# The scans' opening moved into attention's last units: maxima spread, four weight blocks split, head 0's value projections

## The chip, the cores and the metric

The kernel runs on one core of one Trainium2 chip. Its time is the device time of one launch in microseconds (us). Matrix products run on TensorE (PE; its weight loads are shown as PEld), elementwise work and reductions on VectorE (DVE), activations and scaled copies on ScalarE (ACT), some products and masks on GpSimd (POOL), and the transfers are issued by SyncE (SP). PSUM is the eight-bank memory that PE writes (512 fp32 columns a bank), SBUF the working memory.

## The reference

One trunk layer of a hybrid diffusion backbone on 128 context tokens and 1024 latent tokens, model width 1024: a SwiGLU half step, a token mixer, a second SwiGLU half step, each with modulation and a closing layer norm. The change lies in the mixer. It projects its input once and splits the columns into an attention part (8 query heads, 2 key/value heads of 64) and a part for four recurrent heads of 128 (HGRN2, run forward and backward):

```python
def mixer_latent(h, *, k_ctx, v_ctx, s_f0, s_b0, w_in, w_out, q_g, k_g, hg_g, lb_f, lb_b):
    hq, hi, hff, hfb, hgate, aq, ak, av = split_in(h @ w_in)
    o_hg, _, _ = hgrn2_mixer(hq, hi, hff, hfb, hgate, lb_f, lb_b, hg_g, s_f0, s_b0)
    q, k, v = attn_proj(aq, ak, av, q_g, k_g)
    ...
    o_att = block_attention(q, k_all, v_all)
    y = jnp.concatenate([o_hg, o_att.astype(o_hg.dtype)], axis=-1) @ w_out

def hgrn2_mixer(hq, hi, hf_fwd, hf_bwd, hgate, lb_fwd, lb_bwd, norm_g, s_fwd0, s_bwd0):
    q = heads(jax.nn.silu(hq.astype(f32)))
    v = heads(hi.astype(f32))
    # per direction: f = lb + (1 - lb) * sigmoid(hf); gated linear recurrence in chunks of 16 over (q, 1 - f, log f, v)
    ...
    o = rms_norm(o_f + o_b, norm_g.reshape(HG_HEADS, HG_HEAD_DIM)).reshape(b, l, HG_WIDTH)
    o = o * jax.nn.silu(hgate.astype(f32))
```

## The kernel before

The kernel keeps all 1152 tokens in SBUF as nine tiles of 128 and runs in phases, each a block of five hand-written instruction queues: the first half step with the mixer's query, key and value projection and attention, then the scans with the output projection, then the last half step. At the end of a block all engines meet; nothing of the next block runs before that. Within a block the order on each engine is that of the code, and semaphores (`wait_ge`, `then_inc`) tie the engines together.

**Attention** goes through 18 units u (nine query tiles by two key/value heads, `NU` = 18). Units 0 to 15 are latent tiles over ten key tiles; 16 and 17 belong to the context tile and have one key tile each. The queues are pipelined over units: in the iteration of unit u, PE transposes the probabilities of u (`turn`), multiplies them with the values (`values`), computes the scores of u + 1 (`main`, `tails`) and the first of u + 2, and spreads the inverse sums (`inverse_rows`). ACT exponentiates (`exponents`), copies the transposes out as high halves (`probs_hi`), and at the end the inverse rows and the low half of the output (`copy_rows`, `low_half`). DVE takes the minima of the scores (`least`), the low halves (`probs_lo`) and adds the output halves (`add_halves`, semaphore `added`), which PE's next unit and POOL's closing product (L1428) wait for. The transposes share two banks, so each waits for the low half of the one two before. The scores use the first five banks; the context units' scores touch banks 0 and 3 alone.

**The scans** need, for each head, five weight blocks of 128 columns: V (values), F0 and F1 (forget gates of the two directions), Q, and G (output gate). Products are in fp16 in three passes, so each fp32 block is split: the largest absolute value of all partitions gives a power of two, ACT writes the scaled high half (L3070, semaphore `w_hi`), DVE the low half (L3236, `w_lo`). Head 0's blocks are loaded during attention (`load_scan_weights`), and its five per-partition maxima are taken there too (`next_weight_max`, in units 12, 13, 14, 16, 17). At the opening of the scans' block PE spreads the maxima over the partitions (`spread_max`'s form, L2886), DVE reduces them and makes scale and inverse (`power`), the splits V, F0, Q, F1 follow, and PE runs `project`: V in nine units of one tile (24 products of 128 columns each, L2903), the others in three units of 384 columns (24 products each, L2906). Each unit goes to one of two banks, in the order of `ring`, and waits (`left`) until ACT has evacuated the unit two before (L3057 for V, L3061 for the others). For the next head SP loads each raw block as soon as `w_lo` shows the previous split, sends the maxima through DRAM to spread them (`spread_max` on SP: L2800 out, L2802 back), and loads G behind that; DVE's `row_max` waits for four loads at once. ACT's queue has `split(1, V_)`, which waits for head 1's scales (`w_scale`), between the gates' logarithm and Q's evacuations:

```python
            split(0, G_)
            evacuate(0, F0, 0, 1, 2)
            log_gate(0, 0)
            split(1, V_)
            evacuate(0, Q_, 0, 1, 2)
            exps(0, 0)
```

PE's queue in the scans begins with the spread and then waits for `ready`, which POOL raises when it has written zero states, the reset row and two masks (L2843 to L2856).

## Time and profile before

| | us |
|---|---|
| median of 3 runs | 2631.96 |
| lowest and highest run | 2628.84 and 2632.33 |
| the profiled execution, its own time | 2627.32 |
| span of the profiled execution (first to last instruction) | 2625.6 |
| mean granted TensorE clock, share of full speed | 0.97 |

In a row of a timeline the columns are the start, the length, the engine, the line of the kernel, the operation with output and inputs, and its count; in brackets how long the engine stood idle before it, and what ended that. Rows with a count over one merge instructions in a run. The clock column of a stretch is 1.00 at 2.4 GHz and 0.50 at 1.2 GHz.

### The profile page before, as it was taken

What the parts mean: (1) busy time and instruction counts of PE and PEld (TensorE: products, weight loads), DVE (VectorE), ACT (ScalarE), POOL (GpSimd) and SP (SyncE); (2) the same over time, 40 slices, a digit from 0 to 9 for tenths busy, and PEclk for the clock granted to TensorE, in tenths of its full rate; (3) what the DMA queues carried; (4) which work ended last, traced back from release to release, by engine and by line L of the source; (5) the groups of instructions that cost most, each with busy time, mean ns of one, the idle gap of its engine ahead of it and who ended that gap; (6) DMA issues with size and microseconds to landing.
All of it is one profiled execution on the core that took longest, in us unless ns stands there. A gap on an engine that the chain in (4) does not pass through costs nothing. (4 is left out here: it accounts for less than half of the span.)

```text
span 2625.6 us, 38449 instructions
## 1 busy us (share of the span) xinstructions
PE 2451.6 (93%) x15508; PEld 1500.0 (57%) x15508; DVE 1925.7 (73%) x2867; ACT 827.6 (32%) x1313; POOL 186.5 (7%) x220
## 2 busy tenths in 40 slices
PE   7999999999999787999799889899899999999987
PEld 2555555555555466777576666545455555555543
DVE  4687777789576766888648658798877676677687
ACT  2411111111121345777644454623222121122220
POOL 0000000000000022222200000311000000000002
PEclk9999999999999889999899999899999999999998
DMA  8133322331212111000120111231211111111001
GB/s 329 49 113 97 97 83 94 97 113 62 67 36 85 63 37 27 1 1 1 31 67 15 42 45 37 69 102 49 65 48 48 48 33 47 48 48 38 26 25 65
DMA packets 151085, 160.55 MB, mean 61 GB/s; under 512 B 11767, under 2 KB 128403, under 8 KB 149922
## 3 DMA queue, kind: packets, MB, share of 16 engines
q1 hardware_dynamic: 150946, 158.61, 19.1%
q8 instruction: 98, 1.61, 0.3%
q14 instruction: 41, 0.34, 0.0%
HBM read 148.47 MB, written 10.12 MB: 60 GB/s over the span
## 5 line engine op out<-in xcount | busy, mean ns | idle before, releaser
L2010 PE MATMUL psum<-act_hi,ffn_win_hi 128*128 128x384 f16 x2064 | 675.2, 327 | 4.8 <-DVE ffn_win_lo L2334 2.4
L2010 PE MATMUL psum<-act_lo,ffn_win_hi 128*128 128x384 f16 x2064 | 674.8, 327 | 0.0
L2010 PE MATMUL psum<-act_hi,ffn_win_lo 128*128 128x384 f16 x2064 | 674.7, 327 | 0.0
L2210 ACT ACTIVATE ffn_silu<-psum,ffn_win_inverse 128x384 f32<-128x384 f32 x132 | 76.3, 578 | 1061.5 <-PE psum L2010 1057.8
L2402 DVE SCALAR_TENSOR_TENSOR Y<-psum,ffn_h_unit,Y 128x512 f32<-128x512 f32 x324 | 239.8, 749 | 108.2 <-PE psum L2055 106.2
L2055 PE MATMUL psum<-ffn_wout_hi,ffn_h_hi 128*128 128x512 f16 x720 | 278.1, 386 | 7.5 <-issue 5.3
L2010 PEld LDWEIGHTS psum<-act_hi,ffn_win_hi 128*128 128x128 f16 x2064 | 202.5, 98 | 139.1 <-DVE ffn_win_lo L2334 2.8
L2010 PEld LDWEIGHTS psum<-act_hi,ffn_win_lo 128*128 128x128 f16 x2064 | 202.5, 98 | 134.7 <-issue 2.0
L2010 PEld LDWEIGHTS psum<-act_lo,ffn_win_hi 128*128 128x128 f16 x2064 | 202.5, 98 | 133.9 <-issue 1.5
L2055 PE MATMUL psum<-ffn_wout_lo,ffn_h_hi 128*128 128x512 f16 x720 | 277.7, 386 | 0.0
L2055 PE MATMUL psum<-ffn_wout_hi,ffn_h_lo 128*128 128x512 f16 x720 | 277.2, 385 | 0.0
L2367 DVE SCALAR_TENSOR_TENSOR ffn_h_even<-psum,ffn_win_inverse,ffn_silu 128x384 f32<-128x384 f32 x72 | 44.2, 614 | 123.5 <-ACT ffn_silu L2210 123.3
L2055 PEld LDWEIGHTS psum<-ffn_wout_hi,ffn_h_hi 128*128 128x128 f16 x720 | 71.7, 100 | 97.3 <-issue 10.9
L2906 PE MATMUL psum<-act_hi,scan_w_hi 128*128 128x384 f16 x384 | 125.4, 326 | 0.0
L2906 PE MATMUL psum<-act_lo,scan_w_hi 128*128 128x384 f16 x384 | 125.2, 326 | 0.0
L2906 PE MATMUL psum<-act_hi,scan_w_lo 128*128 128x384 f16 x384 | 125.2, 326 | 0.0
L2190 ACT ACTIVATE ffn_win_hi<-ffn_win_raw,ffn_win_scale 128x2048 f16<-128x2048 f32 x44 | 87.7, 1994 | 115.9 <-DVE ffn_win_inverse L2328 90.0
L429 DVE SCALAR_TENSOR_TENSOR mod_sums<-w_mod,silu_cond,mod_sums 128x1024 f32<-128x1024 f32 x98 | 122.8, 1277 | 0.0
L2055 PEld LDWEIGHTS psum<-ffn_wout_hi,ffn_h_lo 128*128 128x128 f16 x720 | 71.5, 99 | 88.1 <-issue 5.7
L1343 DVE TENSOR_REDUCE score_min<-psum 128x1 f32<-128x1280 f32 (+1 forms) x72 | 97.5, 1354 | 33.1 <-PE psum L1136 22.2
L1355 DVE TENSOR_TENSOR probsT_lo<-psum,probsT_hi 128x512 fp32r<-128x512 f32 x162 | 105.5, 683 | 19.7 <-ACT probsT_hi L1274 19.5
L2055 PEld LDWEIGHTS psum<-ffn_wout_lo,ffn_h_hi 128*128 128x128 f16 x720 | 71.6, 99 | 83.3 <-issue 4.6
(379 smaller groups left out, 4298.3 us busy)
## 6 DMA issues: line engine op xcount, KB each, us to landing
ffn_win_raw<-in_w_in SPq DMA_DIRECT2D x88, 512.0 KB, 5.1
w_mod<-in_w_mod SPq DMA_DIRECT2D x36, 1024.0 KB, 5.0
ffn_wout_raw<-in_w_out SPq DMA_DIRECT2D x44, 512.0 KB, 4.1
scan_w_raw<-in_w_mix SPq DMA_DIRECT2D x20, 512.0 KB, 5.3
x_after<-Y SPq DMA_DIRECT2D x9, 512.0 KB, 2.6
mixout_residual<-x_after SPq DMA_DIRECT2D x9, 512.0 KB, 3.5
Y<-in_x_sample SPq DMA_DIRECT2D x8, 512.0 KB, 11.6
ffn_residual<-in_x_sample SPq DMA_DIRECT2D x8, 512.0 KB, 3.3
```

The costliest lines, as they stand in the source:

```text
L429: ins = nc.vector.scalar_tensor_tensor(acc, w, factor, acc, ALU.mult, ALU.add)
L1343: self.nc.vector.tensor_reduce(self.low[:, u % 2, s:s + 1], self.score_view(u, s), AX_X, ALU.min).then_inc(self.s_min, 1)
L1355: nc.vector.tensor_tensor(self.pt[g % self.NPT][1][:], self.T[i % 2], self.pt[g % self.NPT][0][:].bitcast(F32), ALU.subtract).then_inc(sel ...
L2010: last = nc.tensor.matmul(bank[:, 0:CH], win[b][w][:, half, k, :], K.A[a][:, k, c * CH:(c + 1) * CH], start=(n == 0), stop=(n == 3 * KT - 1))
L2055: last = nc.tensor.matmul(py[m % 3], h[a][:, b, t * P:(t + 1) * P], wout[w][:, b, 0 if mod else int(t == CTX_T), half * 512:(half + 1) * 512],
L2190: nc.scalar.activation(win[par][0][:], wraw[par][:], ACT.Copy, scale=ws[:, par:par + 1]).then_inc(in_hi, 1)
L2210: nc.scalar.activation(sa[s][:], pa[s][:, 0:CH], ACT.Silu, scale=winv[:, b:b + 1]).then_inc(silu, 1)
L2367: nc.vector.scalar_tensor_tensor(dst, pu[s][:, 0:CH], winv[:, b:b + 1], sa[s][:], ALU.mult, ALU.mult).then_inc(hprod, 1)
L2402: ins = nc.vector.scalar_tensor_tensor(dst, py[m % 3], hq[:], dst, ALU.mult, ALU.add)
L2906: last = nc.tensor.matmul(proj[u % 2][:, 0:CH], w[x][:, k, :], K.A[y][:, k, i * CH:(i + 1) * CH], start=(m == 0), stop=(m == 3 * KT - 1))
```

## The change

Head 0's opening is taken out of the scans' block, except for block G and the evacuation of the values, and put into attention's last units.

- The maxima of blocks 3 and 4 (Q and G) are taken by DVE in unit 14, right behind that of block 2, in place of units 16 and 17.
- In unit 15 PE spreads the five maxima (`spread_weights`) into banks 1 and 2 ahead of the scores' tail; at the unit's end DVE computes the scales (`next_weights_scale`), ACT the high half of V and DVE its low half.
- In unit 16 PE projects value tiles 0 and 1, 2 and 3, 4 and 5 at three places of its order, in unit 17 tiles 6 and 7 and then 8 (`next_values`), into banks 1, 2 and 4. ACT splits Q, F1's and F0's high halves behind `low_half` of unit 16 (blocks 2, 3, 1), DVE their low halves at the end of its unit 16.
- In the scans' block PE begins with `ready` and F0. ACT evacuates the nine value tiles in three copies (`v_first`), for which F0's second unit waits. `w_lo`, `w_hi` and `w_scale` are raised at once, so SP's loads for head 1 no longer wait for head 0's splits.
- The split weights and the scales get fixed places in SBUF outside what attention uses.

```diff
@@ -1055,6 +1055,8 @@
         self.s_main, self.s_tail, self.s_min, self.ex, self.inverse = (
             sem(n) for n in ("scores", "score_tails", "score_min", "exp", "inverse"))
         self.pv, self.low_out, self.added, self.scaled = sem("pv"), sem("low_copied"), sem("o_added"), sem("o_scaled")
+        self.next_spread, self.next_scale, self.next_hi, self.next_lo, self.next_chain = (
+            sem(n) for n in ("scan_w_spread", "scan_w_scaled", "scan_w_hi", "scan_w_lo", "scan_w_chain"))
         self.next_in, self.next_late, self.next_max = sem("scan_w_loaded"), sem("scan_w_late"), sem("scan_w_max")
         self.tiles = [len(self.keys(u)) for u in range(self.NU)]
         self.first = [sum(self.tiles[:u]) for u in range(self.NU + 1)]
@@ -1164,6 +1166,50 @@
             pe.wait_ge(self.ex, h)
         self.scores(u, 2 * pair, 1024, 1024, 256)
         self.scores(u, 2 * pair + 1, 1280, 0, 256).then_inc(self.s_tail, 1)
+
+    def spread_weights(self, pe):
+
+        K = self.K
+        pe.wait_ge(self.next_max, 5)
+        pe.wait_ge(self.ex, NKV * CTX_T * self.HPK)
+        for b in range(5):
+            last = spread_max(self.nc, K, K.first_spread[:, b * P:(b + 1) * P], K.scan_rmax[:, b:b + 1])
+        last.then_inc(self.next_spread, 1)
+
+    def next_values(self, pe, *tiles):
+
+        K, (hi, lo) = self.K, self.K.scan_W[0]
+        for i in tiles:
+            if i == 0:
+                pe.wait_ge(self.next_lo, 1)
+            bank, n = K.first_v[i // 4][:, (i % 4) * P:(i % 4 + 1) * P], 0
+            for k in range(KT):
+                for x, y in PASSES:
+                    self.nc.tensor.matmul(bank, K.A[x][:, k, i * P:(i + 1) * P], (hi, lo)[y][:, k, :], start=(n == 0), stop=(n == 3 * KT - 1))
+                    n += 1
+
+    def next_weights_hi(self, act, *blocks):
+
+        K = self.K
+        for b in blocks:
+            act.wait_ge(self.qkv.q_steps, self.qkv.ROPE * NT)
+            act.wait_ge(self.next_scale, 1)
+            self.nc.scalar.activation(K.scan_W[b][0][:], K.scan_raw[:, b], ACT.Copy, scale=K.first_ws[:, b:b + 1]).then_inc(self.next_hi, 1)
+
+    def next_weights_lo(self, dve, n, b):
+
+        K = self.K
+        dve.wait_ge(self.next_hi, n + 1)
+        self.nc.vector.scalar_tensor_tensor(K.scan_W[b][1][:], K.scan_raw[:, b], K.first_ws[:, b:b + 1], K.scan_W[b][0][:],
+                                            ALU.mult, ALU.subtract).then_inc(self.next_lo, 1)
+
+    def next_weights_scale(self, dve):
+
+        K, nc, link = self.K, self.nc, Chain(dve, self.next_chain)
+        dve.wait_ge(self.next_spread, 1)
+        link(nc.vector.tensor_reduce(K.first_wmax, K.first_spread.rearrange("p (j q) -> p j q", q=P), AX_X, ALU.max))
+        power_of_two(nc, link, K.first_wmax, K.first_wq, K.first_ws)
+        nc.vector.tensor_scalar(K.first_winv, K.first_wq, K.unit_a[:, 1:2], None, ALU.mult).then_inc(self.next_scale, 1)
 
     def tensor(self, pe):
 
@@ -1216,19 +1262,31 @@
             main(pe, u + 1, 2)
             turn(u, 4)
             turn(u, 5)
+            if u == NU - 3:
+                self.spread_weights(pe)
             tails(pe, u + 1, 1)
+            if u == NU - 2:
+                self.next_values(pe, 0, 1)
+            if u == NU - 1:
+                self.next_values(pe, 6, 7)
             values(u, 0)
             values(u, 1)
             turn(u, 6)
             turn(u, 7)
             values(u, 2)
             main(pe, u + 1, 3)
+            if u == NU - 2:
+                self.next_values(pe, 2, 3)
             values(u, 3)
             values(u, 4)
             self.turn_queries(pe, u + 2)
             turn(u, 8)
             values(u, 5)
             inverse_rows(u)
+            if u == NU - 2:
+                self.next_values(pe, 4, 5)
+            if u == NU - 1:
+                self.next_values(pe, 8)
             main(pe, u + 2, 0)
             tails(pe, u + 2, 0)
             turn(u, 9)
@@ -1311,7 +1369,11 @@
             probs_hi(u + 1, 0)
             self.exponents(act, u + 2, 0)
             probs_hi(u + 1, 1)
+            if u == NU - 3:
+                self.next_weights_hi(act, 0)
             low_half(u)
+            if u == NU - 2:
+                self.next_weights_hi(act, 2, 3, 1)
 
     def keys_lo(self, dve, kv, b):
 
@@ -1401,8 +1463,15 @@
             self.least(dve, u + 2, 0)
             if u in (12, 13, 14):
                 next_weight_max(u - 12)
-            elif u in (16, 17):
-                next_weight_max(u - 13)
+                if u == 14:
+                    next_weight_max(3)
+                    next_weight_max(4)
+            if u == NU - 3:
+                self.next_weights_scale(dve)
+                self.next_weights_lo(dve, 0, 0)
+            elif u == NU - 2:
+                for n, b in ((1, 2), (2, 3), (3, 1)):
+                    self.next_weights_lo(dve, n, b)
         add_halves(NU - 1)
 
     def pool(self, gp):
@@ -2652,9 +2721,10 @@
     with ExitStack() as ctx:
         sem = lambda n: K.semaphore(f"scan_{n}")
         raw, rmax = K.scan_raw, K.scan_rmax
-        W = [[place(f"scan_w_{s}_{x}", [P, KT, P], F16) for x in ("hi", "lo")] for s in range(5)]
+        W = K.scan_W
+        place.at += 5 * 4096
         wmax, wq = place("scan_w_max", [P, 5]), place("scan_w_unit", [P, 5])
-        ws, winv = ([place(f"scan_w_{n}_{i}", [P, 5]) for i in range(2)] for n in ("scale", "inverse"))
+        ws, winv = ([first, place(f"scan_w_{n}", [P, 5])] for n, first in (("scale", K.first_ws), ("inverse", K.first_winv)))
         spread = place("scan_w_max_spread", [P, 5 * P])
         q = place("scan_q", [P, TOK])
         reset = place("scan_reset", [P, CH])
@@ -2693,7 +2763,7 @@
         stored, chain, pchain = sem("states_stored"), sem("chain"), sem("pool_chain")
         mix_in = [sem(f"mixout_w_loaded_{i}") for i in range(3)]
         mix_parts = ((0, 2, 3), (1, 4), (5, 6, 7))
-        first_max, w_turned = K.wide[3][:, 0:5 * P], sem("first_w_max_spread")
+        v_first = sem("first_v")
         w_max, w_stored, w_spread, w_scale = sem("w_max"), sem("w_max_stored"), sem("w_max_loaded"), sem("w_scaled")
         wv = K.w_mix[0].rearrange("(k p) n -> p k n", p=P)
 
@@ -2705,7 +2775,7 @@
         RPH = 6
         CPT = P // SCAN
 
-        ring = [(0, b, i) for b in (V_, F0, Q_, F1) for i in range(COUNT[b])]
+        ring = [(0, b, i) for b in (F0, Q_, F1) for i in range(COUNT[b])]
         for h in range(HGH):
             n = h + 1
             parts = [[(n, V_, i) for i in range(6)], [(h - 1, "norm", i) for i in (2, 1, 0)], [(n, V_, i) for i in range(6, NT)],
@@ -2882,10 +2952,6 @@
 
         @block.tensor
         def _(pe):
-            for b in range(NBLK):
-                last = nc.tensor.matmul(first_max[:, b * P:(b + 1) * P], rmax[:, b:b + 1].broadcast_to([P, P]), K.ident[:],
-                                        start=True, stop=True)
-            last.then_inc(w_turned, 1)
             pe.wait_ge(ready, 1)
 
             def project(n, b, *units):
@@ -2939,7 +3005,7 @@
             def updates(h, d, r):
                 R = h * RPH + 3 * d + r
                 pe.wait_ge(kb_s, R + 1)
-                if d == 0 and r == 0:
+                if h and d == 0 and r == 0:
                     pe.wait_ge(left, ring_at[h, V_, NT - 1] + FREE + 1)
                 if R:
                     pe.wait_ge(st_s, R)
@@ -3028,8 +3094,10 @@
                     turn(n, 0, 0)
                 project(n, F1, 2)
 
-            project(0, V_, *range(NT))
-            for b in (F0, Q_, F1):
+            project(0, F0, 0)
+            pe.wait_ge(v_first, 3)
+            project(0, F0, 1, 2)
+            for b in (Q_, F1):
                 project(0, b, 0, 1, 2)
             for h in range(HGH):
                 scan_head(h)
@@ -3038,6 +3106,11 @@
         @block.scalar
         def _(act):
             act.sem_inc(left, FREE)
+            act.sem_inc(w_hi, 4)
+            for i, bank in enumerate(K.first_v):
+                tiles = slice(4 * i, min(4 * i + 4, NT))
+                nc.scalar.activation(v[0][:, tiles, :].rearrange("p t k -> p (t k)"), bank, ACT.Copy,
+                                     scale=winv[0][:, V_:V_ + 1]).then_inc(v_first, 1)
             act.wait_ge(lbs, 1)
             for d in range(2):
                 nc.scalar.activation(lb[:, 0, d, :], K.lbd[:, d, :], ACT.Sigmoid)
@@ -3065,7 +3138,7 @@
                 if n >= HGH:
                     return
                 act.wait_ge(w_scale, 1 if n == 0 else 2 * n + (b == G_))
-                if n:
+                if n and (n, b) != (1, V_):
                     act.wait_ge(acc_p, ring_at[n - 1, b, COUNT[b] - 1] + 1)
                 nc.scalar.activation(W[b][0][:], raw[:, b], ACT.Copy, scale=ws[n % 2][:, b:b + 1]).then_inc(w_hi, 1)
 
@@ -3203,11 +3276,6 @@
                 squares(h, 1)
                 split_out.outputs_hi(act, 3, 4)
 
-            split(0, V_)
-            split(0, F0)
-            split(0, Q_)
-            split(0, F1)
-            evacuate(0, V_, *range(NT))
             split(0, G_)
             evacuate(0, F0, 0, 1, 2)
             log_gate(0, 0)
@@ -3437,15 +3505,11 @@
                 split(n + 1, Q_)
                 split(n + 1, F1)
 
-            dve.wait_ge(w_turned, 1)
-            power(0, 0, NBLK, first_max.rearrange("p (j q) -> p j q", q=P))
+            dve.sem_inc(w_scale, 1)
+            dve.sem_inc(w_lo, 4)
             dve.wait_ge(lbs, 2)
-            split(0, V_)
             link(nc.vector.tensor_scalar(lb[:, 2], lb[:, 1], -1.0, None, ALU.mult))
             columns(0)
-            split(0, F0)
-            split(0, Q_)
-            split(0, F1)
             row_max(1, 0, V_, F0, Q_, F1).then_inc(w_max, 1)
             split(0, G_)
             row_max(1, 1, G_).then_inc(w_max, 1)
@@ -3510,10 +3574,16 @@
     K.scan_rmax = K.unit_a[:, 3:8]
     K.mix_raw = [nc.alloc_sbuf_tensor_at(f"mixout_w_raw_{k}", [P, D], F32, offset=SCAN_RAW_AT + 4096 * k if k < 5 else mix_at + 4096 * (0, 2, 3)[k - 5])
                  for k in range(KT)]
+    K.scan_W = [[nc.alloc_sbuf_tensor_at(f"scan_w_{b}_{x}", [P, KT, P], F16, offset=mix_at + 4096 * b + 2048 * i)
+                 for i, x in enumerate(("hi", "lo"))] for b in range(5)]
+    K.first_wq, K.first_ws, K.first_winv = (K.cols[:, C_BMOD + 56 + 5 * i:C_BMOD + 61 + 5 * i] for i in range(3))
+    K.first_wmax = K.cols[:, C_C:C_C + 5]
     K.mix_omax, K.mix_wmax, K.mix_wq, K.mix_ws = (K.cols[:, C_BMOD + i * KT:C_BMOD + (i + 1) * KT] for i in range(4))
     with ExitStack() as ctx:
         psum = ctx.enter_context(nc.psum_tensor("psum", [P, 4096], F32))
         K.score_banks = psum[:, 0:2560]
+        K.first_spread = psum[:, 512:512 + 5 * P]
+        K.first_v = [psum[:, 512:1024], psum[:, 1024:1536], psum[:, 2048:2048 + P]]
         K.wide = [psum[:, 1024 * i:1024 * (i + 1)] for i in range(4)]
         banks = [psum[:, 512 * i:512 * (i + 1)] for i in range(8)]
         K.mod_rows = nc.dram_tensor("mod_rows", (2, N_MOD * D), F32).ap()
```

## Rows read from the trace of the kernel before

**Rows 1.** The page: busy time of each engine, share of the span, instructions.
```profile
PE 2451.6 (93%) x15508; PEld 1500.0 (57%) x15508; DVE 1925.7 (73%) x2867; ACT 827.6 (32%) x1313; POOL 186.5 (7%) x220
```

**Rows 2.** Busy time by stretch, attention's last units: length, busy per engine, clock, DMA.
```profile
1284.00:1297.00 13.00, 7.63 (x43) 5.53 (x40) 7.39 (x15) 6.99 (x17) 2.91 (x4) 0.87 0.00 1
```

**Rows 3.** Timeline of all engines across the boundary from attention to the scans.
```profile
1297.55 1.51 POOL L1428 TENSOR_TENSOR mix_out_T<-pv_sum,inverse_rows 64x256 f32<-64x256 f32 x2 [2.58 <-DVE pv_sum L1374]
...
1300.69 0.20 POOL L2843 MEMSET zero_state<- 128x128 f32 x1 [1.63 <-POOLq L3487]
...
1300.73 2.48 PE L2886 MATMUL psum<-ident,act_units 128*128 128x128 f32 x10 [5.35 <-PEq L3487]
...
1303.24 0.83 DVE L3248 TENSOR_REDUCE scan_w_max<-psum 128x5 f32<-128x640 f32 x1 [5.93 <-PE psum L2886]
...
1304.19 0.29 POOL L2856 TENSOR_SCALAR_AFFINE_SELECT mask<-mask 128x128 f32<-128x128 f32 x1
...
1305.03 3.23 ACT L3070 ACTIVATE scan_w_hi<-scan_w_raw,scan_w_scale 128x1024 f16<-128x1024 f32 x3 [2.48 <-DVE scan_w_inverse L3250]
...
1307.71 0.26 PE L2903 MATMUL psum<-scan_w_hi,act_hi 128*128 128x128 f16 x1 [4.50 <-issue]
```

**Rows 4.** Timeline of ACT in the scans' opening.
```profile
1310.46 0.37 ACT L3057 ACTIVATE scan_v<-psum,scan_w_inverse 128x128 f32<-128x128 f32 x1 [1.17 <-PE psum L2903]
1311.97 0.37 ACT L3057 ACTIVATE scan_v<-psum,scan_w_inverse 128x128 f32<-128x128 f32 x1 [1.14 <-PE psum L2903]
...
1321.35 0.37 ACT L3057 ACTIVATE scan_v<-psum,scan_w_inverse 128x128 f32<-128x128 f32 x1 [0.97 <-PE psum L2903]
...
1325.25 0.58 ACT L3061 ACTIVATE scan_buf<-psum,scan_w_inverse 128x384 f32<-128x384 f32 x1 [2.50 <-PE psum L2906]
...
1336.20 1.13 ACT L3070 ACTIVATE scan_w_hi<-scan_w_raw,scan_w_scale 128x1024 f16<-128x1024 f32 x1
1337.35 1.28 ACT L3061 ACT_TABLE_LOAD   x1
1338.64 0.58 ACT L3061 ACTIVATE scan_q<-psum,scan_w_inverse 128x384 f32<-128x384 f32 x1
```

**Rows 5.** Timeline of DVE, attention's last units and the scans' opening.
```profile
1271.12 1.21 DVE L124 TENSOR_REDUCE act_units<-scan_w_raw 128x1 f32<-128x1024 f32 x1
1272.24 1.28 DVE L1355 TENSOR_TENSOR probsT_lo<-psum,probsT_hi 128x512 fp32r<-128x512 f32 x2
...
1285.53 1.45 DVE L1355 TENSOR_TENSOR probsT_lo<-psum,probsT_hi 128x512 fp32r<-128x512 f32 x2 [0.80 <-ACT probsT_hi L1274]
...
1292.62 0.68 DVE L1374 TENSOR_TENSOR pv_sum<-psum,pv_low_half 64x512 f32<-64x512 f32 x1
...
1308.97 3.67 DVE L3236 SCALAR_TENSOR_TENSOR scan_w_lo<-scan_w_raw,scan_w_scale,scan_w_hi 128x1024 f16<-128x1024 f32 x3 [0.16 <-DVE head_cols L3265]
1319.67 4.60 DVE L124 TENSOR_REDUCE act_units<-scan_w_raw 128x1 f32<-128x1024 f32 x4 [7.03 <-DMA scan_w_raw<-in_w_mix]
...
1334.65 0.23 DVE L3250 TENSOR_SCALAR scan_w_inverse<-scan_w_unit,act_units 128x4 f32<-128x4 f32 x1
```

**Rows 6.** Timeline of PE in attention's last units.
```profile
1273.27 0.60 PE L1179 MATMUL psum<-ident,probs 128*128 128x128 f32 x4
...
1286.84 0.39 PE L1191 MATMUL psum<-probsT_hi,v_hi_lo 128*128 128x512 f32 x1
...
1288.94 0.47 PE L1191 MATMUL psum<-probsT_hi,v_hi_lo 128*128 128x512 f32 x1 [1.09 <-DVE pv_sum L1374]
...
1290.69 0.66 PE L1179 MATMUL psum<-ident,probs 128*128 128x128 f32 x4 [0.44 <-ACT probs L1259]
1293.45 0.65 PE L1191 MATMUL psum<-probsT_hi,v_hi_lo 128*128 128x512 f32 x1 [2.10 <-DVE pv_sum L1374]
```

**Rows 7.** Timeline of SP's DMA issues in the scans' opening.
```profile
1307.63 5.41 SPq L2791 DMA_DIRECT2D scan_w_raw<-in_w_mix  x4
...
1326.10 0.44 SPq L2791 DMA_DIRECT2D scan_w_raw<-in_w_mix  x1
```

## The prediction

> **What bounds the kernel now.** I read the page first: TensorE (PE) is busy for 93% of the span [rows 1], so in most stretches a microsecond saved elsewhere is worth nothing, and a gain has to come from a place where PE stands still. The table by stretches names one that the change touches: in the last 13.0 us of attention PE is busy for 7.63 us [rows 2]. The timeline of all engines across the phase boundary shows the other. GpSimd's last product of attention starts at 1297.55 and lasts 1.51, the next phase's first instructions stand at 1300.69, and PE's first value projection (L2903) at 1307.71. Between lies one chain: ten fp32 passes spreading the five maxima (2.48 us, to 1303.21), VectorE's (DVE's) reduction and powers of two (1303.24 to 1305.03), ScalarE's (ACT's) first high half and DVE's low half [rows 3]. The reader should see two separate things in these rows: a chain of about 7.0 us from the phase's start to PE's first projection, and GpSimd's masks, which end at 1304.48, 3.8 us into the phase. PE waits for those too (`ready`), and today that is covered by the chain.
>
> From there PE runs without a gap through V, F0, Q and F1 of head 0. The values' evacuations show V's price: the first comes 2.75 us after PE's start, then 1.51, then 1.34 for each of the last seven tiles ((1321.35 - 1311.97)/7), so nine tiles cost 13.6 us, of which 1.5 is TensorE at the lower of its two clock levels after its pause. A unit of the other blocks takes 3.90 us (from the last value tile's evacuation at 1321.35 to F0's first at 1325.25) [rows 4]. F0 starts at 1321.3, and nine such units, 35.1 us, bring F1's end to 1356.4. I measure everything from the phase's start, S (1300.69 before): F0 starts at S + 20.6, F1 ends at S + 55.7.
>
> **What leaves the opening.** The spread, the scales, four weight splits and nine value tiles go. F0 then waits only for `ready`, at about S + 3.85 by GpSimd's rows [rows 3]; ACT's three copies of the values out of PSUM (one of 512 columns of this sort costs about 0.6) lie within it and hold only F0's second unit. The pause before it is as long as before, so I keep the slow start of 1.4 to 1.5 us. That is 20.6 - 3.85 - 1.4 = 15.35 us less.
>
> **What attention gains in length**, along its path.
> - *Unit 14*: DVE takes two more maxima in the same place. One lasts 1.21 alone, and four in a row take 4.60, so two add 2.3. The low half behind them starts at 1272.24, ends its first part about 0.35 before PE's transpose at 1273.27 needs its bank [rows 5, 6]: 2.0 us. The two maxima taken away (units 16 and 17) lay where DVE waited; nothing comes back.
> - *Unit 15, spread*: ten passes at the full clock, half of 2.48, 1.2 us of PE ahead of transposes that PE works through in order. Together 3.2.
> - *Unit 15, end*: DVE is free at 1284.73 (1285.53 less its idle 0.80 [rows 5]). Shifted that is 1287.95. Now come reduction and powers (1.79), ACT's high half (1.15, ACT being behind an exponent), DVE's low half (1.25): until 1292.2. Only then come the low halves of the last transposes of unit 15, whose value product PE started at 1286.84 and can now start at about 1292.85. That is 6.0 us late, with PE waiting for some 2.8 us.
> - *Unit 16*: before, 3.85 us pass from that product to the transposes of unit 17 (1290.69) [rows 6]. Now six value tiles stand between them, 6 x 1.34 = 8.05, with what PE has there anyhow: two products at 0.47, three scores at about 0.2, the inverse rows at 0.4, 1.9 in all. A pause of 2.10 us came out at the slow clock (0.65 for a product at 1293.45), one of 1.09 did not (0.47 at 1288.94) [rows 6]; with a pause of 2.8 I take the slow clock and 1.4 us for it. So 11.35, 7.5 more: unit 17's transposes are 13.5 late.
> - *End of unit 16*: ACT copies the high half and the low output half, and only behind these stand its three weight high halves (1.15 for the first). DVE's three low halves (3.67) stand ahead of unit 17's low half (0.65) and of the addition which PE and GpSimd wait for. From the transposes to that addition took 1.93 (1290.69 to 1292.62 [rows 5, 6]); now 1.9 + 1.2 + 3.67 + 0.65 = 7.4. That is 5.5 more, 19.0 in all. Tiles 6 and 7 run on PE meanwhile, tile 8 beside the last inverse rows; without that cover they would cost 2.7 and 1.3.
> - The rest, addition to GpSimd's end, keeps its length. S moves from 1300.69 to 1319.7.
>
> So 12.1 us of projections are bought with 19.0 us of attention: the addition's chain of ACT and DVE is exposed where PE was.
>
> **What goes wrong after F0.** The loads for head 1 start at once, as `w_lo` is already raised: four issues, the last at S + 2.3. Before, they were issued over 5.41 us from 1307.63 and DVE's maxima began at 1319.67 [rows 5, 7]: 7.0 us from the last issue, 12.0 from the first. That gives bounds of S + 9.3 and S + 12.8; they overlap from the first and only shared before, so I take S + 10. From the landing to head 1's scales took 15.2 us (1319.67 to 1334.88 [rows 5]): maxima, a round trip through DRAM, and load G queued behind that round trip on SP (issued at 1326.10 [rows 7], 1.8 us after the maxima's end at 1324.27). All of this keeps its order, so the scales are there at S + 25.2. ACT's queue has head 1's V split ahead of Q's evacuations. PE has Q's second unit done at S + 3.85 + 1.4 + 5 x 3.9 = S + 24.75, but Q's third needs the bank of the first, and ACT evacuates it only after the split, a table load and the copy, 3.0 us from 1336.20 to 1339.22 [rows 4]: S + 28.3. PE stands 3.5 us, resumes slowly, 1.4 more: 4.9 us. Before, the scales were 1.3 us early (1334.88 against 1336.20), so this wait did not exist; afterwards the sums, exponents and products of head 0 end at about S + 43, before F1 ends, and cost nothing. F1 ends at S + 3.85 + 1.4 + 35.1 + 4.9 = S + 45.3, against S + 55.7: a gain of 10.4.
>
> A rule of the Trainium skill bears on that wait. In these rows the table load starts at 1337.35 and the next activation at 1338.64, 1.29 us later [rows 4]. "ScalarE: Activation LUTs", section "What ACT_TABLE_LOAD costs", has about 1.38 us of draining on top of such a load. By it the wait would be longer by that, and the sum 1.4 larger. The trace shows no such drain, and the measured 1.29 is used.
>
> **The sum.** +19.0 - 10.4 = +8.6 us. Everything behind F1 keeps its order and moves with it. The profiled execution took 2627.32 us, 1.7 more than its span of 2625.6, so it would become 2635.9. It lies 4.6 below the median of the runs shown (2631.96), on which the prediction stands: 2640.5.
>
> Bounds: no slow clock in unit 16, -1.4; none at Q, -1.4; landing at S + 9.3 or S + 12.8, -0.7 or +2.8; spread half hidden, -0.6; the splits' hand-overs longer, +1. Together +4.5 to +12.4.
>
> **Rivals.**
> 1. *No wait at Q*: if the four loads land about 3.5 us sooner than I take, below my floor, or the scales' chain is shorter. For it: the engines' 2.1 MB move with nothing else beside them. Against: the 7.0 and 12.0 us of rows 5 and 7. Then +8.6 - 4.9 = +3.7, 2635.7: within 0.2%, 5.3 us, about what a measurement of this kernel can tell from no change.
> 2. *Not slower: attention's splits hide.* If the weight splits do not hold up DVE's queue (PE's tiles cover them, whatever the order), the terms of 2.8 at the end of unit 15, 1.4 of clock and 5.5 at unit 16's end fall away. Attention then grows by 19.0 - 9.7 = 9.3 us and the sum is -1.1: 2630.9. The idle share of PE at attention's end [rows 2] speaks for it; the order of the queues, in which the splits stand ahead of work that PE waits for, against. It decides where attention grows by less than 10.4. For a gain above 0.2% it has to grow by less than 5.1, or lose rival 1's wait as well: 2626.
> 3. *Worse*: the loads land at the late bound, and one of the later hand-overs (products of head 0, then the transposes) slips behind F1 by two or three us: +13 to +15, 2646.
> 4. *The skill's drain is real*, +10.0 in all, 2642. The trace's 1.29 speaks against it.
>
> **How the numbers follow.** My forecast 0.60 (its own range +4.5 to +12.4, nearly all above 5.3), rival 1 0.15, rival 2 0.14, rival 3 0.08, rival 4 0.03. The range reaches from rival 2 to between the forecast and rival 3: 2631 to 2646. Slower by over 0.2%: the forecast's 0.55, rivals 3 and 4, together 0.66. Faster by over 0.2%: the lower part of rival 2 and an overlap with 1, 0.08. Same: the rest, 0.26.
>
> **What the changed profile would show.** GpSimd's last attention product about 19 us later (near 1316.5); DVE maxima three in a row at unit 14; PE idle about 2.8 us before the last value product of unit 15 and some 4 to 5 us before unit 17's; DVE idle for ACT's high halves; F0's first matmul 3.9 us after the phase begins; a PE gap of 3 to 4 us ahead of Q's third unit with ACT waiting for head 1's scales; F1 ending near S + 45. If attention grows by under 12 us, or the gap at Q is missing, the prediction fails at that term.

## The result, and the profile after

| | before | after |
|---|---|---|
| median, 12 runs each, us | 2630.87 | 2637.66 |
| lowest and highest run | 2628.51, 2632.33 | 2633.77, 2644.53 |
| the profiled execution, its own time | 2627.32 | 2639.85 |
| its span | 2625.6 | 2638.1 |
| its mean granted TensorE clock | 0.970 | 0.968 |

The changed kernel is slower: 1.0031 times the time of before, 95% interval 1.0023 to 1.0038, so 8.2 us (6.0 to 10.0) on 2630.87. The two medians alone differ by 6.8. The forecast was +8.6 and 2640.5.

Not all of the 12.5 us between the two profiled spans belongs to the change. DVE's maxima of unit 14 begin at 1271.12 before [rows 5] and at 1273.68 after, and up to there the two kernels run the same code. I therefore measure both traces from that instruction, the anchor, and inside the scans from S, the first instruction of their block.

First the page of the changed kernel, the busy times that answer to [rows 1].

```profile
PE 2458.7 (93%) x15508; PEld 1501.2 (57%) x15508; DVE 1926.1 (73%) x2867; ACT 826.8 (31%) x1307; POOL 186.7 (7%) x220
```

PE is busy for 7.1 us longer over the same 15508 products and its share is what it was. A busy time that grows while the work does not is the clock. 1.8 of the 7.1 us lie before the anchor and 5.0 between it and the first masked weights of head 0; over that second stretch the changed kernel takes 10.1 us more, so the other 5.1 are standing time. Next its timeline of PE; the rows up to 1315.29 answer to [rows 6].

```profile
1277.80 0.66 PE L1225 MATMUL psum<-ident,probs 128*128 128x128 f32 x4 [1.79 <-DVE probsT_lo L1417]
...
1282.92 1.28 PE L119 MATMUL psum<-ident,act_units 128*128 128x128 f32 x10
...
1295.55 0.51 PE L1237 MATMUL psum<-probsT_hi,v_hi_lo 128*128 128x512 f32 x1 [2.60 <-DVE probsT_lo L1417]
...
1307.34 0.61 PE L1225 MATMUL psum<-ident,probs 128*128 128x128 f32 x4
...
1315.29 0.76 PE L1237 MATMUL psum<-probsT_hi,v_hi_lo 128*128 128x512 f32 x1 [4.66 <-DVE pv_sum L1436]
...
1326.58 0.50 PE L2972 MATMUL psum<-act_hi,scan_w_hi 128*128 128x384 f16 x1 [6.69 <-POOLq L2928]
...
1351.79 0.50 PE L2972 MATMUL psum<-act_hi,scan_w_hi 128*128 128x384 f16 x1 [3.73 <-ACT scan_q L3134]
```

Four gaps can be read in it: 1.79 us behind unit 14's maxima, 2.60 before the last value product of unit 15, 4.66 before the first product of unit 17, and 3.73 in the scans, released by ACT's evacuation of Q (`scan_q`). The ten spreading passes take 1.28 us at full clock.

The timeline of DVE, to be read beside [rows 5].

```profile
1273.68 3.46 DVE L124 TENSOR_REDUCE act_units<-scan_w_raw 128x1 f32<-128x1024 f32 x3
...
1293.61 1.28 DVE L1203 SCALAR_TENSOR_TENSOR scan_w_lo<-scan_w_raw,param_cols,scan_w_hi 128x1024 f16<-128x1024 f32 x1 [1.30 <-ACT scan_w_hi L1197]
...
1310.27 3.67 DVE L1203 SCALAR_TENSOR_TENSOR scan_w_lo<-scan_w_raw,param_cols,scan_w_hi 128x1024 f16<-128x1024 f32 x3 [7.55 <-ACT scan_w_hi L1197]
1313.87 0.68 DVE L1417 TENSOR_TENSOR probsT_lo<-psum,probsT_hi 128x512 fp32r<-128x512 f32 x1
1314.47 0.67 DVE L1436 TENSOR_TENSOR pv_sum<-psum,pv_low_half 64x512 f32<-64x512 f32 x1
...
1333.30 4.60 DVE L124 TENSOR_REDUCE act_units<-scan_w_raw 128x1 f32<-128x1024 f32 x4 [5.67 <-DMA scan_w_raw<-in_w_mix]
...
1348.42 0.23 DVE L3318 TENSOR_SCALAR scan_w_inverse<-scan_w_unit,act_units 128x4 f32<-128x4 f32 x1
```

The three weight low halves at 1310.27 wait 7.55 us for ACT and stand ahead of the low half at 1313.87 and the addition at 1314.47, which PE's 4.66 us end on. In the scans DVE stands 5.67 us for head 1's loads.

The timelines of ACT (beside [rows 4]), of POOL and of SP's queue (beside [rows 3] and [rows 7]).

```profile
1309.09 3.23 ACT L1197 ACTIVATE scan_w_hi<-scan_w_raw,param_cols 128x1024 f16<-128x1024 f32 x3
...
1348.69 1.15 ACT L3143 ACTIVATE scan_w_hi<-scan_w_raw,scan_w_scale 128x1024 f16<-128x1024 f32 x1 [5.15 <-DVE scan_w_inverse L3318]
1349.86 1.28 ACT L3134 ACT_TABLE_LOAD   x1
1351.15 1.05 ACT L3134 ACTIVATE scan_q<-psum,param_cols 128x384 f32<-128x384 f32 x2
...
1358.74 0.58 ACT L3134 ACTIVATE scan_q<-psum,param_cols 128x384 f32<-128x384 f32 x1 [6.54 <-PE psum L2972]
...
1370.44 0.58 ACT L3134 ACTIVATE scan_buf<-psum,param_cols 128x384 f32<-128x384 f32 x1 [3.32 <-PE psum L2972]
```

```profile
1319.50 1.51 POOL L1497 TENSOR_TENSOR mix_out_T<-pv_sum,inverse_rows 64x256 f32<-64x256 f32 x2 [2.71 <-DVE pv_sum L1436]
1322.67 0.20 POOL L2913 MEMSET zero_state<- 128x128 f32 x1 [1.65 <-POOLq L3551]
```

```profile
1323.53 4.25 SPq L2861 DMA_DIRECT2D scan_w_raw<-in_w_mix  x4
...
1339.72 0.43 SPq L2861 DMA_DIRECT2D scan_w_raw<-in_w_mix  x1
```

S is 1322.67. SP's four loads are issued over 4.25 us, G only at 1339.72. ACT waits 5.15 us for head 1's scales (`scan_w_inverse`), then splits V, reloads its table and only then evacuates Q at 1351.15. Then come 6.54 us for one unit of Q: PE worked without a gap, but ran 18 of its 24 products at the low level of the clock. The table by stretches shows the clock (columns as in [rows 2]) behind the gap of 1.79 us, in attention's end, and in Q's third unit.

```profile
1277.80:1280.30 2.50, 2.50 (x14) 2.02 (x15) 1.43 (x3) 1.57 (x3) 0.00 (x0) 0.76 0.00 0
```

```profile
1293.00:1316.00 23.00, 15.79 (x212) 15.34 (x213) 8.99 (x13) 7.42 (x14) 2.16 (x3) 0.87 0.01 1
1351.80:1370.40 18.60, 18.60 (x98) 10.56 (x99) 8.87 (x12) 8.13 (x10) 0.00 (x0) 0.84 0.21 61
```

PE has no gap in the first and the third of them and still loses, at 0.76 and at 0.84: the 18.60 us hold the slow unit of Q and the three units of F1 at full pace. In the 23.00 us of attention it is busy for 15.79.

### The profile page after: what moved, and what is told of

The parts are those of the page before. It is cut to its first block and busy times, and to the rows that moved or that the text cites. A ratio compares the mean times of both kernels' runs of the same rounds, so it can differ in the third digit from the quotient of the medians.

```text
span 2638.1 us, 38448 instructions
## 1 busy us (share of the span) xinstructions
PE 2458.7 (93%) x15508; PEld 1501.2 (57%) x15508; DVE 1926.1 (73%) x2867; ACT 826.8 (31%) x1307; POOL 186.7 (7%) x220
```

## The experiments

Every kernel below computes all that the reference asks for. They are the changed kernel with one or more of five edits:

- *Order of DVE*: the three low halves of unit 16 stand behind the addition that PE waits for.
- *Q first*: ACT splits head 1's V behind Q's evacuations.
- *G early*: head 1's G is loaded ahead of the maxima's way through DRAM, and DVE splits G of head 0 ahead of those maxima.
- *Order of unit 15*: scales and V's halves stand behind unit 15's own low halves, and the first four value tiles behind the scores of unit 17.
- *Masks late*: PE waits for POOL's `ready` behind F0's first unit.

Times are medians of 11 or 12 runs (e3 has 6, e6 7 and e10 5); the ratio is to runs of before taken together with them. "S" is measured from the anchor (before 29.57, after 48.99), "scales" (head 1's scales are there) and "F1" (the start of its last evacuation) from S. "Late" is how much later than before, from the anchor, the first masked scan weights of head 0 and the last masked weights of the scans come. S, scales, F1 and lateness are each read from one profiled execution.

| kernel | median | ratio, 95% | S | scales | F1 | late, first and last |
|---|---|---|---|---|---|---|
| before | 2630.87 | | 29.57 | 34.2 | 55.8 | 0, 0 |
| after | 2637.66 | 1.0031 (1.0023 to 1.0038) | 48.99 | 26.0 | 47.8 | 10.1, 10.2 |
| e1: order of DVE | 2633.87 | 1.0015 (1.0006 to 1.0024) | 45.09 | 26.8 | 48.5 | 7.0, 7.0 |
| e2: Q first | 2635.16 | 1.0016 (1.0008 to 1.0025) | 48.48 | 26.4 | 42.4 | 5.9, 4.0 |
| e3: values back in the scans | 2639.97 | 1.0044 (1.0029 to 1.0059) | 42.30 | 27.6 | 53.0 | 10.1, 10.1 |
| e4: G early | 2637.2 | 1.0023 (1.0014 to 1.0032) | 48.96 | 23.8 | 42.7 | 6.5, 6.6 |
| e5: e1 and e2 | 2633.53 | 1.0014 (1.0006 to 1.0023) | 45.01 | 26.4 | 42.5 | 2.1, 5.6 |
| e6: e1 and order of unit 15 | 2637.52 | 1.0032 (1.0018 to 1.0046) | 46.20 | 26.5 | 47.7 | 8.3, 10.5 |
| e7: e5, e6 and G early | 2633.42 | 1.0013 (1.0004 to 1.0022) | 46.20 | 23.6 | 41.4 | 2.4, 5.6 |
| e8: e7 and masks late | 2627.73 | 0.9993 (0.9984 to 1.0002) | 46.89 | 23.2 | 39.3 | -0.5, 2.3 |
| e9: e8 without order of unit 15 | 2633.68 | 1.0012 (1.0003 to 1.0020) | 45.00 | 23.1 | 39.2 | -1.1, 2.1 |
| e10: masks late alone | 2642.7 | 1.0034 (1.0021 to 1.0047) | 49.00 | 26.6 | 48.1 | 11.1, 13.8 |

**e1, the low halves behind the addition.** In DVE's queue of unit 16 and 17:

```diff
-            elif u == NU - 2:
-                for n, b in ((1, 2), (2, 3), (3, 1)):
-                    self.next_weights_lo(dve, n, b)
...
             if u:
                 add_halves(u - 1)
+            if u == NU - 1:
+                for n, b in ((1, 2), (2, 3), (3, 1)):
+                    self.next_weights_lo(dve, n, b)
```

> The changed kernel, with DVE's three weight low halves of unit 16 moved behind unit 17's low half and the addition of unit 16. Theory (the splits stand ahead of work that PE waits for): unit 17's low half starts about 5 us sooner, GpSimd's last attention product as well, since ACT's high halves and DVE's low halves then lie beside PE's last value tiles; the time falls from +8 against the kernel before to about +3 us. Rival (the low halves only move to the next wait, ahead of the last addition): GpSimd's end moves by under 1 us and the time stays near +8.

The timeline of DVE in e1:

```profile
1309.50 0.69 DVE L1417 TENSOR_TENSOR probsT_lo<-psum,probsT_hi 128x512 fp32r<-128x512 f32 x1 [5.89 <-ACT probsT_hi L1332]
1310.11 0.68 DVE L1436 TENSOR_TENSOR pv_sum<-psum,pv_low_half 64x512 f32<-64x512 f32 x1
1311.16 4.44 DVE L1203 SCALAR_TENSOR_TENSOR scan_w_lo<-scan_w_raw,param_cols,scan_w_hi 128x1024 f16<-128x1024 f32 x3 [0.37 <-ACT scan_w_hi L1197]
1315.53 0.67 DVE L1436 TENSOR_TENSOR pv_sum<-psum,pv_low_half 64x512 f32<-64x512 f32 x1
```

The addition at 1310.11 now stands ahead of the splits, PE's 4.66 us are gone, and S comes at 45.09 from the anchor instead of 48.99: 3.9 us, of the 5.5 that the forecast put on this order. Up to unit 17's transposes the two kernels need the same 33.7 us from the anchor, so all of the 3.9 lie behind them. About 1 us of the rest stays because the last addition (1315.53) now stands behind the splits: ACT's low half for it ends at 1314.59. Whole time and lateness follow (1.0031 to 1.0015; 10.1 to 7.0).

**e2, Q's evacuations first.**

```diff
-            split(1, V_)
             evacuate(0, Q_, 0, 1, 2)
+            split(1, V_)
```

> The changed kernel, with ACT's split of head 1's V block behind Q's three evacuations instead of ahead of them. Theory (PE stands because ACT waits for head 1's scales with Q's first unit unevacuated): PE's gap of 3.7 us before Q's third unit is gone and its slow unit too (3.9 instead of 7.0 us from the evacuation before), F1 ends near S + 41 to S + 42 instead of S + 47.7, the time is at +2 to +3 us against the kernel before. Rival (the products of head 0 become the next limit, as their exponents still wait for the same scales): F1 ends early but the transposes of head 0 wait, and under 2 us are won: +6 or more.

The timeline of ACT in e2:

```profile
1340.72 0.58 ACT L3134 ACTIVATE scan_q<-psum,param_cols 128x384 f32<-128x384 f32 x1
...
1348.34 1.14 ACT L3143 ACTIVATE scan_w_hi<-scan_w_raw,scan_w_scale 128x1024 f16<-128x1024 f32 x1
...
1360.97 0.58 ACT L3134 ACTIVATE scan_buf<-psum,param_cols 128x384 f32<-128x384 f32 x1 [3.69 <-PE psum L2972]
```

Q's evacuations come at PE's pitch and F1 ends at S + 42.4 instead of 47.8. The forecast had priced that wait at 4.9; taking it away is worth 5.3, net of a new wait of 1.23 us: the split at 1348.34 now stands ahead of F1's evacuations. By the ratio the time is at +4.2 us, where +2 to +3 had been expected.

**e4, the loads' and DVE's order.** SP's and DVE's queues:

```diff
             load(1, F1)
+            sp.wait_ge(w_lo, split_at[0, G_] + 1)
+            sp.dma_start(raw[:, G_], ...).then_inc(g_in, 16)
             spread_max(1, 0)
-            load(1, G_)
...
-            row_max(1, 0, V_, F0, Q_, F1).then_inc(w_max, 1)
             split(0, G_)
+            row_max(1, 0, V_, F0, Q_, F1).then_inc(w_max, 1)
```

> The changed kernel, with load G of head 1 issued ahead of the round trip of the maxima (with a semaphore of its own), and DVE's low half of head 0's G ahead of the maxima. Theory (the scales of head 1 come late because load G stands behind the round trip, and DVE's maximum of G ahead of the scales): the scales are there at about S + 23 instead of S + 26.0, PE's gap at Q shrinks from 3.7 us to under 1, the time is at about +3 to +4 us. Rival (loads and maxima alone set the scales): they come no earlier than S + 25 and the time stays near +8.

Its timelines of DVE and of PE:

```profile
1331.82 5.72 DVE L124 TENSOR_REDUCE act_units<-scan_w_raw 128x1 f32<-128x1024 f32 x5 [5.01 <-DMA scan_w_raw<-in_w_mix]
...
1343.94 0.23 DVE L3322 TENSOR_SCALAR scan_w_inverse<-scan_w_unit,act_units 128x4 f32<-128x4 f32 x1
```

```profile
1347.30 0.34 PE L2973 MATMUL psum<-act_hi,scan_w_hi 128*128 128x384 f16 x1 [1.50 <-ACT scan_q L3135]
```

And the stretch behind that gap (columns as in [rows 2]):

```profile
1347.30:1351.40 4.10, 4.10 (x26) 2.48 (x27) 3.71 (x8) 0.42 (x1) 0.00 (x0) 1.00 0.00 0
```

The scales come 2.2 us sooner, so PE waits 1.50 instead of 3.73. The first product behind the wait lasts 0.34 and not 0.50, and the clock stays at 1.00: this pause did not bring the low level. That is why 2.2 us of scales bring 5.1 us at F1's end. e2 removes the wait and e4 shortens it by other means, and both end at S + 42.4 to 42.7: the wait, and not the split's own work, is what held Q. The scales were expected at S + 23, the gap under 1 and the time at +3 to +4 us; the time is at +6.0 (3.7 to 8.4), and its interval overlaps that of the changed kernel, so the gain is shown in the trace alone.

**e3, the value projections back in the scans,** with maxima, spread, scales and splits left in attention. The diff shows one of the `next_values` calls; all of them go.

```diff
-            if u == NU - 2:
-                self.next_values(pe, 0, 1)
...
-            project(0, F0, 0)
-            pe.wait_ge(v_first, 3)
-            project(0, F0, 1, 2)
-            for b in (Q_, F1):
+            project(0, V_, *range(NT))
+            for b in (F0, Q_, F1):
                 project(0, b, 0, 1, 2)
```

> The changed kernel, with head 0's value projections back at the head of PE's queue in the scans, through the two projection banks; maxima, scales and the four splits stay in attention's last units. Theory (the queues' order costs attention some 12 us whether PE projects there or not): attention's end is about 12 us late, the phase's start to F1's end takes about 53 us, no gap at Q, and the time is again about +8 to +9 us against the kernel before: the moved projections bring what they cost. Rival (the projections lengthen attention, the splits hide beside them): attention's end is late by under 5 us, and the time is between -1 and +2 us.

The timeline of PE in e3:

```profile
1308.69 0.77 PE L1237 MATMUL psum<-probsT_hi,v_hi_lo 128*128 128x512 f32 x1 [7.34 <-DVE pv_sum L1426]
...
1319.97 0.29 PE L2959 MATMUL psum<-scan_w_hi,act_hi 128*128 128x128 f16 x1 [9.24 <-POOLq L2918]
```

S comes 6.7 us sooner (42.30) and the opening up to F1 is 5.2 us longer; the other 1.5 go behind F1, and the lateness is 10.1 as before the edit. The ratio 1.0044 (1.0029 to 1.0059, from six runs) can't be told apart from 1.0031 (1.0023 to 1.0038). So moving nine tiles, 12.1 us of PE's work, gains nothing by itself: it adds 6.7 to attention, where they partly fill a wait that is there anyhow (without them the gap before unit 17's product is 7.34 us instead of 4.66), and takes little more from the opening, where they had filled the time until Q is evacuated. The other 12.7 of attention's 19.4 us are maxima, spread and splits.

**e10 and e9, the wait for the masks.** The edit, alone in e10:

```diff
-            pe.wait_ge(ready, 1)
...
             project(0, F0, 0)
             pe.wait_ge(v_first, 3)
+            pe.wait_ge(ready, 1)
```

> The changed kernel with one edit: PE's wait for GpSimd's masks behind F0's first unit. Theory (F1's end is set by head 1's scales, for which ACT holds Q's evacuations): F0 ends 3.8 us sooner, PE's gap before Q's third unit grows from 3.7 to some 7.5 us, F1 still ends at S + 47 to S + 48, and the time stays at +8. Rival (each wait is a term by itself): F1 ends near S + 44, +4.5.

Its timeline of PE:

```profile
1322.72 0.34 PE L2970 MATMUL psum<-act_hi,scan_w_hi 128*128 128x384 f16 x1 [3.06 <-DVEq L3508]
...
1352.13 0.50 PE L2970 MATMUL psum<-act_hi,scan_w_hi 128*128 128x384 f16 x1 [8.07 <-ACT scan_q L3133]
```

PE starts F0 at S + 0.3 instead of S + 3.9, and the gap before Q's third unit grows from 3.73 to 8.07. The path from S to Q runs over the loads and scales of head 1, and what PE saves ahead of it is waited for there. With Q's evacuations first and G early the same edit does count (41.4 to 39.3 in F1's end, between e7 and e8).

> The kernel of the run before without the new order of units 15 to 17: low halves behind, load G early, Q's evacuations first, the wait for GpSimd's masks ahead of F0's second unit. Theory (the new order cost 1 to 2 us, as PE then stands ahead of all four value tiles and does them at the slow clock): the phase starts 45.1 us after the maxima of unit 14 instead of 46.9, F1 ends near S + 39, and the time is 1 to 2 us below that of the run before: -3 to -4 us, -0.1 to -0.15%, against the kernel before. Rival (what is left is set by where TensorE's clock falls after each pause in the four heads, not by the opening): the opening is shorter by these 1.8 us and the time is the same or worse.

e9 has S at 45.00 and F1's end at S + 39.2, 2.0 us sooner altogether than e8 (0.6 by the first masked weights), and yet its median is 6.0 us above (5.0 by the ratios). The order of unit 15 does cost the opening what the theory said, but the forecast of -3 to -4 us failed (+3.2): the rival, by which a shorter opening gives the same time or a worse one, describes what came. This is taken up below.

**e5 to e8, the edits together.**

> The first two experiments' edits together on the changed kernel: the three low halves behind unit 17's low half and addition, and ACT's V split of head 1 behind Q's evacuations. Theory (the two waits are separate terms of one sum): both savings add, some 4 and 5 to 6 us, and of the loss of 8 to 10 nothing is left: -2 to +1 us against the kernel before. Rival (a common limit behind both, such as the sums and exponents of head 0): the two together are worth no more than one, +3 to +4.

> The first experiment's edit, and V's scale and halves in unit 15 to 16 behind attention's own: DVE takes unit 15's last low halves, then the scales, the addition of unit 15, then V's low half; ACT V's high half behind the low output half; PE the first four value tiles in one piece behind unit 17's last scores. Theory (V's split ahead of unit 15's last low halves held PE up for 2.6 us and let its clock fall): attention ends 2 to 3 us sooner than with the first edit alone (whose phase starts 45.1 us after the maxima of unit 14), so 42 to 43 us, and the time is at +1 to +2. Rival (PE waits for V's low half instead, at the value tiles, for as long): 45 us and +4.

> All edits so far together: low halves behind, the order of units 15 to 17, load G early, Q's evacuations first. Theory: attention's end as in the run before (42 to 43 us from the maxima of unit 14), F1's end near S + 41, no PE gap over 1.5 us between F0 and F1, the time -3 to -5 us against the kernel before. Rival (the clock is slow for longer after each pause, or the limit moves to head 0's sums): within 2 us of the kernel before.

> The kernel of the run before, and PE's wait for GpSimd's masks moved from ahead of F0 to ahead of its second unit. Theory (PE stands for 3.85 us at the phase's start for masks that it needs only after F1): F0's first unit starts near S + 0.1, F1 ends near S + 38, the time falls by a further 2 to 3.5 us, to about -6 us or -0.25%. Rival (the factors of head 0, which depend on head 1's loads through DVE's queue, come at S + 37 to S + 39 in any case): F1 ends sooner but PE then waits for them before it turns head 0, and under 1 us is won.

Against before, the ratios put these four at +3.7, +8.4, +3.4 and -1.8 us, where -2 to +1, +1 to +2, -3 to -5 and about -6 had been expected. All four forecasts of the whole time were too favourable; e5 stands where its rival put it, though by another cause than the common limit that the rival named.

e6's edit, in DVE's and PE's queues (ACT's high half of V also goes behind `low_half`, which is not shown):

```diff
             probs_lo(u, 0)
+            if u == NU - 2:
+                self.next_weights_scale(dve)
             probs_lo(u, 1)
...
             if u:
                 add_halves(u - 1)
+            if u == NU - 2:
+                self.next_weights_lo(dve, 0, 0)
...
-                self.next_values(pe, 2, 3)
+                self.next_values(pe, 0, 1, 2, 3)
```

The timeline of PE in e6:

```profile
1292.99 0.47 PE L1237 MATMUL psum<-probsT_hi,v_hi_lo 128*128 128x512 f32 x1 [1.68 <-DVE pv_sum L1434]
...
1302.93 0.60 PE L1245 MATMUL psum<-ident,prob_sum_inverse 128*64 128x128 f32 x4
```

And a stretch between the two:

```profile
1295.00:1300.00 5.00, 5.00 (x48) 5.00 (x49) 0.57 (x3) 0.92 (x4) 0.48 (x1) 0.50 0.00 0
```

The pause of 2.60 us before unit 15's last product is gone. In its place PE waits 1.68 us for the addition of unit 15, before the first product of unit 16 (the row at 1292.99), and S comes at 46.20, 1.1 later than in e1. From that product to the inverse rows of unit 16 pass 9.9 us: PE goes through four tiles, now in one piece, without a gap, but for 5.00 us at 0.50, the lower level, which is 2.5 us lost. What the queues gave, the clock took; the cause of this stretch was not tested further.

Up to the first masked weights the edits add up: e1 takes off 3.1 and e2 4.2 alone, e5 8.0 together, and e8 is 0.5 us earlier there than before. The whole time does not follow. e5 is 2.1 us late at the first masked weights and 5.6 at the last, e7 2.4 and 5.6, e8 -0.5 and 2.3, e9 -1.1 and 2.1, e6 8.3 and 10.5, e10 11.1 and 13.8, e2 5.9 and 4.0, while after, e1, e3 and e4 keep their lateness to 0.1. So up to 3.4 us come or go in code that no edit touches. PE's waits don't show them. Here are the two largest of 330 us from head 0's first masked weights, first of before, then of e5; the columns are the line, what it waited for, and us in total, times, longest.

```profile
PE psum L2935 <- ACT ke_turned L3093: 18.4, 8, 5.8
PE psum L2903 <- ACT scan_v L3057: 7.7, 2, 3.9
```

```profile
PE psum L3001 <- ACT ke_turned L3166: 18.4, 8, 5.8
PE psum L2969 <- ACT scan_v L3130: 7.7, 2, 3.9
```

The waits are the same to a tenth, as are the next three of the list. What differs is the clock. The stretch from the first masked weights to the last, in before, e5 and e2 (columns as in [rows 2]):

```profile
1366.05:1685.50 319.45, 284.16 (x3014) 208.53 (x3014) 235.01 (x497) 151.88 (x273) 30.60 (x35) 0.95 0.10 30
```

```profile
1371.09:1693.95 322.86, 287.50 (x3014) 211.70 (x3014) 235.08 (x497) 151.40 (x273) 30.05 (x35) 0.94 0.10 30
```

```profile
1370.87:1688.36 317.49, 282.18 (x3014) 206.73 (x3014) 235.02 (x496) 152.15 (x273) 30.98 (x35) 0.96 0.10 30
```

PE does the same 3014 products in all three and stands for 35.3 to 35.4 us. Its busy time is 284.2, 287.5 and 282.2 us, at 0.95, 0.94 and 0.96: the whole difference is the clock. A place where it arises: the same pause of 3.86 us, once in before and once in e8 (timeline of PE):

```profile
1456.22 0.23 PE L2903 MATMUL psum<-scan_w_hi,act_hi 128*128 128x128 f16 x1 [3.86 <-ACT scan_v L3057]
```

```profile
1456.69 0.29 PE L2967 MATMUL psum<-scan_w_hi,act_hi 128*128 128x128 f16 x1 [3.86 <-ACT scan_v L3129]
```

And the 5.00 us behind the pause (columns as in [rows 2]), in before, in e8 and in e2, which has the same pause of 3.86 us ahead of 1461.22:

```profile
1456.22:1461.22 5.00, 5.00 (x62) 4.55 (x63) 2.00 (x3) 1.43 (x5) 0.00 (x0) 0.66 0.47 137
```

```profile
1456.69:1461.69 5.00, 5.00 (x46) 4.78 (x50) 1.72 (x2) 1.43 (x5) 0.00 (x0) 0.50 0.16 48
```

```profile
1461.22:1466.22 5.00, 5.00 (x89) 4.76 (x90) 3.40 (x7) 1.84 (x7) 0.00 (x0) 1.00 0.42 121
```

Before resumes at full speed and falls to the low level 1.2 us later, so it goes through at 0.66; e8 is at the low level at once, 0.50; e2 never falls. In the scans, then, what comes or goes is TensorE's clock and no wait. Why the slow stretches lie where they do in each kernel, the rows don't show.

From the last masked weights to the end it is otherwise. Before takes 940.1 us there, and after, e1, e3, e4, e6 and e10 are within 0.5 of that; e8 takes 0.3 us more, e5, e7 and e9 2.2 more, and e2 4.8 more. PE is busy for no longer in e2, e5, e7 and e9 than in before (895.9 to 898.6 us against 898.8), but it stands longer: two of its waits for DVE in the last phase come to 6.4 us against 4.8 and to 3.5 against 1.8. No run tests what lengthens them.

## Why the prediction was right

**The outcome.** Forecast +8.6, measured +8.2 by the ratio (6.0 to 10.0); forecast time 2640.5, median 2637.66, inside the range. From the anchor to the first masked weights the trace has +10.1. Term by term:

| step | forecast | in the trace |
|---|---|---|
| two more maxima in unit 14 | +2.0 | +2.0 (PE's wait before the transposes 2.15 to 4.12 from the maxima's start) |
| with the spread of unit 15 | +3.2 | +3.4 |
| unit 15's last value product | +6.0 | +6.2 |
| PE's gap there | 2.8 | 2.60 |
| slow clock in unit 16 | 1.4 | 1.6 (against e1, which goes from unit 15's last product to unit 17's transposes at full clock) |
| unit 17's transposes | +13.5 | +14.1 |
| addition of unit 16 | +19.0 | +19.3 |
| S | +19.0 | +19.4 |
| F0's start | S + 3.85 | S + 3.9 |
| head 1's loads landed | S + 10 | S + 10.6 |
| scales | S + 25.2 | S + 26.0 |
| PE's gap at Q | 3.5 | 3.73 |
| slow clock behind the gaps before F0 and at Q | 1.4 and 1.4 | 2.0 and 3.05 |
| F1's end | S + 45.3 | S + 47.8 |
| sum at F1's end | +8.6 | +11.4 |

**What held.** Attention's 19.0 came out at 19.4. e1 shows that the three low halves' place in DVE's queue is one cause (3.9), and e3 that the tiles add 6.7 there (the forecast had 7.5 for them with their slow clock) and give back no more than that. The wait at Q, which did not exist before, came at its place and at its length; e2 removes it, e4 shortens it to 1.50 us, and each gains 5 us at F1's end, and e10 shows that PE's start on F0 does not count as long as it stands. A unit of 384 columns kept its pitch of 3.90.

**What was mis-sized.** The term "resumes slowly, 1.4 more". It was read off V's first tiles [rows 4], a single stretch. After the gap at Q three quarters of the unit stayed at the low level: 18 of its 24 products last 0.50 to 0.53 instead of 0.33, and the third unit took 6.95 us for 3.90, 3.05 more. After the longer pause before F0 it was 2.0. The landing is the smaller miss: I had the four loads issued by S + 2.3, while SP took 4.25 us over them, to S + 5.1, and the scales came 0.8 late. The prediction names no row for the S + 2.3, and [rows 7] had 5.41 us for the same four issues. Together the two misses are 2.4 us at F1's end. The 2.0 before F0 count for nothing, as they lie within the wait at Q. About 1.3 us came back before the first masked weights. There both kernels pause for 3.03 us ahead of one of head 1's value tiles; before resumes at the low level and is at 0.50 for the next 2 us, the changed kernel stays at 1.00 (timelines of PE, before and after):

```profile
1362.45 0.29 PE L2903 MATMUL psum<-scan_w_hi,act_hi 128*128 128x128 f16 x1 [3.03 <-ACT scan_v L3057]
```

```profile
1376.44 0.23 PE L2969 MATMUL psum<-scan_w_hi,act_hi 128*128 128x128 f16 x1 [3.03 <-ACT scan_v L3130]
```

So the closeness of the number is partly luck, as misses of opposite sign met: the slow clock cost more in the opening, another slow stretch fell away, and the runs' median lies below what the trace shows (+8.2 by the ratio against +10.1 at the first masked weights and +9.9 at the end).

**The rivals.** No wait at Q (+3.7): ruled out by the 3.73 us. Splits that hide in attention (-1.1): attention grew by 19.4. Worse by 13 to 15: no further hand-over slipped. The drain behind a table load: ACT's load at 1349.86 is followed by the next activation at 1351.15, 1.29 us later, as before in [rows 4]. So where "ScalarE: Activation LUTs" of the Trainium skill, section "What ACT_TABLE_LOAD costs", adds about 1.38 us of draining, this trace again has none.

**What stays open.** The spread of the changed kernel's runs is 10.8 us, that of before 3.8, and they go roughly by granted clock: those at 0.969 lie between 2633.77 and 2637.78, those at 0.966 and 0.967 between 2643.21 and 2644.53, and the three at 0.968 at 2634.48, 2639.85 and 2640.22. Which slow stretches a variant gets sets up to 3.4 us of its time in the scans, as far as one profiled execution of each can say. Why e8 (0.9993, 0.9984 to 1.0002) beats e9 (1.0012, 1.0003 to 1.0020), whose opening is the shorter one, stays open too. Of the 3.2 us between their profiled spans, 1.4 lie before the anchor and 1.9 behind the last masked weights, while opening and scans cancel; the medians are further apart than that, and no run separates what sets the slow stretches or the longer waits. None of the kernels is shown to be faster than before.

## What to carry to other kernels

Work put into the idle time of an engine has to be placed behind what others wait for in that engine's queue: nine projections cost the same in either place, while three small conversions ahead of one addition cost 3.9 us. Before shortening a chain, ask which transfer or chain of the next step will be late against it; here removing 15 us of opening uncovered a wait of 3.7 us and 3.05 more of slow clock. And where a kernel has many pauses of some microseconds, a change of a few tenths of a per cent can't be predicted from durations alone, as each pause moved may bring or spare a slow stretch that costs 1.3 to 3 us.
